# Hybrid encoder layer on one core: head norms for three tiles at a time, rotations four tiles later, a new order on ScalarE and TensorE, and another split of the output projection

## The reference

```
h = x @ w_in                                     # (n, 1024) x (1024, 3328)
qa, ka, va, ga, qb, kb, vb, gb = split(h)        # A: 4 x 512; B: 512, 128, 128, 512
A: 8 heads of 64; q, k rotated by position; three dilated windows as one masked softmax; times silu(ga)
B: qb, kb = axial_rope(rms_norm_per_head(.))     # 8 query heads, 2 key/value heads
   dense softmax attention per 128 queries; times silu(gb)
f = concat(A, B) @ w_out                         # (n, 1024) x (1024, 1024)
y = layer_norm(2 ** 0.25 * x + f)
```

## Time and profile before

| what | us |
|---|---|
| runs shown (median, lowest, highest) | 535.59, 535.48, 537.15 |
| the profiled execution | 535.67 |
| its span, first to last instruction | 533.8 |
| TensorE busy | 442.6 |
| VectorE busy | 321.6 |
| GpSimd busy | 243.9 |
| ScalarE busy | 223.0 |
| mean granted TensorE clock | 0.94 |

### The profile page before, as it was taken

How to read it: one execution, slowest core, us unless ns; L and a number is a source line. 1 busy time by engine, 2 the same in 40 slices (tenths; PEclk the granted TensorE clock), 3 DMA queues, 4 the chain that set the end, 5 groups by cost and what they waited for, 6 DMA issues and landing times.

```text
span 533.8 us, 8372 instructions
## 1 busy us (share of the span) xinstructions
PE 442.6 (83%) x2956; PEld 404.3 (76%) x2956; DVE 321.6 (60%) x858; ACT 223.0 (42%) x515; POOL 243.9 (46%) x358
## 2 busy tenths in 40 slices
PE   2999764099989797999999897999698979897980
PEld 2989764078889787999988886899597868686860
DVE  2585645574556665656566656555366646563997
ACT  3433111024655454465555454456356745341000
POOL 1277666564325354543425355463344945530111
PEclk9999968589999999999999999999899979898895
DMA  7522111012202011020201011002510050010122
GB/s 258 218 62 61 41 38 41 20 39 60 60 20 62 1 40 41 21 60 20 61 10 52 20 41 41 6 16 69 170 60 21 2 177 20 26 55 1 40 92 106
DMA packets 22586, 29.97 MB, mean 56 GB/s; under 512 B 1936, under 2 KB 16400, under 8 KB 22544
## 3 DMA queue, kind: packets, MB, share of 16 engines
q1 hardware_dynamic: 22112, 29.30, 17.2%
q10 hardware_dynamic: 432, 0.13, 0.1%
HBM read 26.28 MB, written 3.15 MB: 55 GB/s over the span
## 4 chain that ended last, share of the span: by engine, by line
DVE 34%; PE 27%; issue 14%; ACT 12%; POOL 9%; DMA 3%; SPq 1%; DVEq 0%; ACTq 0%; POOLq 0%
PE bank L559 6%; PE bank L561 6%; PE bank L560 6%; DVE prob L897 5%; DVE tmp_s L813 4%; PE bank L521 4%; PE bank L634 4%; ACT p_hi L749 4%; DVE h L859 3%; DVE p_lo L905 3%; POOL scr L1066 3%; ACT prob L740 3%; DVE h L834 2%; DVE q_st L911 2%; DVE o_lo L925 2%
## 5 line engine op out<-in xcount | busy, mean ns | idle before, releaser
L559 PE MATMUL bank<-w_hi,t_lo 128*128 128x256 f32 (+1 forms) x528 | 172.0, 326 | 36.7 <-DVE h L834 12.0
L561 PE MATMUL bank<-w_hi,t_hi 128*128 128x256 f32 (+1 forms) x528 | 163.9, 310 | 0.0
L560 PE MATMUL bank<-w_lo,t_hi 128*128 128x256 f32 (+1 forms) x528 | 163.6, 310 | 0.0
L559 PEld LDWEIGHTS bank<-w_hi,t_lo 128*128 128x128 f32 x528 | 104.3, 197 | 46.9 <-DVE h L834 14.1
L740 ACT ACTIVATE prob<-prob,nmax 128x512 f32<-128x512 f32 (+1 forms) x96 | 62.4, 650 | 149.5 <-DVE nmax L897 149.5
L1056 POOL TENSOR_TENSOR w_lo<-raw,w_hi 128x512 fp32r<-128x512 f32 x59 | 76.1, 1290 | 87.5 <-ACT w_hi L694 87.5
L560 PEld LDWEIGHTS bank<-w_lo,t_hi 128*128 128x128 f32 x528 | 104.3, 197 | 4.6
L561 PEld LDWEIGHTS bank<-w_hi,t_hi 128*128 128x128 f32 x528 | 103.9, 197 | 4.4
L905 DVE TENSOR_TENSOR p_lo<-bank,p_hi 128x512 fp32r<-128x512 f32 x80 | 55.2, 690 | 82.9 <-ACT p_hi L749 82.3
L1103 POOL TENSOR_SCALAR prob<-prob,den 128x512 f32<-128x512 f32 (+1 forms) x96 | 59.3, 623 | 84.1 <-DVE den L918 84.1
L694 ACT ACTIVATE w_hi<-raw 128x512 fp32r<-128x512 f32 x67 | 41.7, 626 | 37.5 <-DMA raw<-w_in 31.3
(11 more groups left out here) (78 smaller groups left out, 704.7 us busy)
## 6 DMA issues: line engine op xcount, KB each, us to landing
raw<-w_in SPq DMA_DIRECT2D x51, 256.0 KB, 2.8
raw<-w_out SPq DMA_DIRECT2D x16, 256.0 KB, 4.2
h<-x_prompt SPq DMA_DIRECT2D x10, 256.0 KB, 3.7
y_prompt<-h SPq DMA_DIRECT2D x8, 256.0 KB, 2.0
h<-x_prompt SPq DMA_DIRECT2D x3, 512.0 KB, 8.4
h<-x_sample SPq DMA_DIRECT2D x2, 512.0 KB, 11.2
h<-x_sample SPq DMA_DIRECT2D x4, 256.0 KB, 5.2
y_sample<-h SPq DMA_DIRECT2D x4, 256.0 KB, 2.0
```

The source lines that it names most:

```text
L559: nc.tensor.matmul(out, a_lo, b_hi, start=(m == 0), stop=False)
L560: nc.tensor.matmul(out, a_hi, b_lo, start=False, stop=False)
L561: ins = nc.tensor.matmul(out, a_hi, b_hi, start=False, stop=end)
```

## The change

In the lead-in, GpSimd makes the reciprocal roots of three tiles by one set of six instructions over 6 or 12 columns a row; tile n is rotated in place n + 4, behind the sums of that place; the lead-in has 22 places, so that all four items of GB0 lie in it. In the steps, ScalarE runs the copies of the transposed heads and probabilities ahead of the exponential, and TensorE transposes the probabilities ahead of all its atoms of the step. OB sums three blocks of rows instead of four, OA five instead of four, and four of the five run early for the first four OA items.

```diff
-ALONE = 17
+ALONE = 19
-EARLY_K = 3
+EARLY_K = 4
+OB_TILES, OA_TILES = (4, 5, 6), (7, 0, 1, 2, 3)
...
         def rotations(place):
-            n = len(norms_of)
-            return {0: (), 1: (), 2: (0,), 3: (1, 2)}.get(place, (place - 1,) if place <= n else ())
+            n = place - NORM_TILES - 1
+            return (n,) if 0 <= n < len(norms_of) else ()
...
@@ tensor, step u @@
-                before = (len(plan[u]) + 1) // 2
-                for i, m in plan[u][:before]:
-                    accumulate(i, m)
                 for b in steps[u]:
                     t_batch(b)
                 if LAG <= u < NU + LAG:
                     prob_transposes(u - LAG)
-                for i, m in plan[u][before:]:
+                for i, m in plan[u]:
                     accumulate(i, m)
...
@@ scalar, step u @@
-                if u < NU:
-                    exps(u)
                 for b in steps[u]:
                     t_high(b)
                 if LAG <= u < NU + LAG:
                     prob_high(u - LAG)
+                if u < NU:
+                    exps(u)
...
@@ vector, sums and lead-in @@
-                if n >= 2:
-                    dve.wait_ge(rstd_ready, n - 1)
-                nc.vector.reduce_sum(ssq[:, n % 2, 0:m], heads_of(squares), axis=AX.X).then_inc(summed, 1)
+                g, k = divmod(n, NORM_TILES)
+                if g >= 2:
+                    dve.wait_ge(rstd_ready, g - 1)
+                nc.vector.reduce_sum(ssq[:, g % 2, k, 0:m], heads_of(squares), axis=AX.X).then_inc(summed, 1)
...
+                if KIND[items[i][0]] == NORM:
+                    sums(i)
                 for n in rotations(i):
                     norm_and_rotate(n)
-                if KIND[items[i][0]] == NORM:
-                    sums(i)
...
@@ gpsimd @@
-            def head_rstd(n):
-                m = norm_heads(norms_of[n][0])
-                pool.wait_ge(summed, n + 1)
-                if n >= 2:
-                    pool.wait_ge(products_ready, n - 1)
-                v, y = ssq[:, n % 2, 0:m], scr[:, 0:m]
+            def head_rstd(g):
+                m = norm_heads(norms_of[NORM_TILES * g][0])
+                pool.wait_ge(summed, NORM_TILES * (g + 1))
+                if g >= 2:
+                    pool.wait_ge(products_ready, NORM_TILES * (g - 1))
+                v, y = ssq[:, g % 2, :, 0:m], scr[:, :, 0:m]
...
+                if KIND[items[i][0]] == NORM and i % NORM_TILES == NORM_TILES - 1:
+                    head_rstd(i // NORM_TILES)
                 for n in rotations(i):
                     add_rotation(n)
-                if KIND[items[i][0]] == NORM:
-                    head_rstd(i)
```

More of the change, by code:

```diff
@@ L62 @@
 PRING = 4
+NORM_TILES = 3
 LAG = 3
@@ L185, in build @@
         den = sb("den", [P, 2, TILES])
[L186 to L189, removed]
+        ssq = sb("ssq", [P, 2, NORM_TILES, 4])
+        rstd = sb("rstd", [P, 2, NORM_TILES, 4])
+        scr = sb("scr", [P, NORM_TILES, 4])
+        half = sb("half", [P, NORM_TILES, 4])
         zero = sb("zero", [P, 1])
@@ L253, in build @@
         parts = [4 if KIND[c] == GATE else TILES for c in range(CHUNKS)]
-        k_tiles = [list(range(KT)) if c < IN_CHUNKS else list(range(KT // 2, KT)) if c in (OB0, OB1)
-                   else list(range(KT // 2)) for c in range(CHUNKS)]
+        k_tiles = [list(range(KT)) if c < IN_CHUNKS else list(OB_TILES) if c in (OB0, OB1) else list(OA_TILES)
+                   for c in range(CHUNKS)]
         items = [(c, n) for c in range(OA0) for n in range(parts[c])]
@@ L661, in _ @@
             for i in range(OA_ITEMS, len(items)):
-                for _, m in atoms_of(i, range(EARLY_K, KT // 2) if i < OA_ITEMS + EARLY else None):
+                for _, m in atoms_of(i, range(EARLY_K, len(OA_TILES)) if i < OA_ITEMS + EARLY else None):
                     accumulate(i, m)
@@ L855, in norm_and_rotate @@
                 m = norm_heads(c)
-                dve.wait_ge(rstd_ready, n + 1)
+                g, place = divmod(n, NORM_TILES)
+                dve.wait_ge(rstd_ready, g + 1)
                 src = h[:, t, HOME[c]:HOME[c] + m * HEAD_DIM]
@@ L859, in norm_and_rotate @@
                 after(nc.vector.tensor_tensor(heads_of(src), heads_of(src),
-                                              rstd[:, n % 2, 0:m, None].to_broadcast([P, m, HEAD_DIM]), ALU.mult))
+                                              rstd[:, g % 2, place, 0:m, None].to_broadcast([P, m, HEAD_DIM]), ALU.mult))
                 rotate(src, src, cos[:, k, :], sin[:, k, :], m, HEAD_DIM // 2, ropes.index((c, t)))
@@ L1057, in weights_low @@
                                         ALU.subtract).then_inc(w_lo_pool, 1)
-            def head_rstd(n):
-                m = norm_heads(norms_of[n][0])
-                pool.wait_ge(summed, n + 1)
-                if n >= 2:
-                    pool.wait_ge(products_ready, n - 1)
-                v, y = ssq[:, n % 2, 0:m], scr[:, 0:m]
+            def head_rstd(g):
[4 more added lines that the diff above has]
+                v, y = ssq[:, g % 2, :, 0:m], scr[:, :, 0:m]
                 after(nc.gpsimd.tensor_scalar(v, v, 1.0 / HEAD_DIM, RMS_EPS, ALU.mult, ALU.add))
-                after(nc.gpsimd.tensor_tensor(y, v, half[:, 0:m], ALU.pow))
-                newton(rstd[:, n % 2, 0:m], v, y).then_inc(rstd_ready, 1)
+                after(nc.gpsimd.tensor_tensor(y, v, half[:, :, 0:m], ALU.pow))
+                newton(rstd[:, g % 2, :, 0:m], v, y).then_inc(rstd_ready, 1)
             def add_rotation(n):
@@ L1118, in _ @@
                     weights_low(g)
+                if KIND[items[i][0]] == NORM and i % NORM_TILES == NORM_TILES - 1:
+                    head_rstd(i // NORM_TILES)
                 for n in rotations(i):
                     add_rotation(n)
-                if KIND[items[i][0]] == NORM:
-                    head_rstd(i)
-                if i == TILES:
+                if i == TILES + NORM_TILES + 1:
                     double_keys(0)
-                if i == TILES + 1:
+                if i == TILES + NORM_TILES + 2:
                     split_values(0)
@@ L1146, in _ @@
                 pool.wait_ge(stats_ready, t + 1)
-                nc.gpsimd.tensor_tensor(lnr[:, t, 3:4], lnr[:, t, 2:3], half[:, 0:1], ALU.pow).then_inc(ln_pow, 1)
+                nc.gpsimd.tensor_tensor(lnr[:, t, 3:4], lnr[:, t, 2:3], half[:, 0, 0:1], ALU.pow).then_inc(ln_pow, 1)
 def kernel(**inputs):
```

## The result

| | before | after |
|---|---|---|
| median of the runs (lowest to highest) | 536.35 us (535.48 to 537.15) | 460.3 us (457.19 to 462.06) |
| the profiled execution, its span | 535.67, 533.8 us | 457.19, 455.2 us |
| first score | 119.20 | 91.52 |
| steps, from the first score to the last part | 371.9 us | 320.7 us |
| last part, to the end of the span | 42.7 us | 43.0 us |

The time is 0.8576 of the time before, with a 95% interval of 0.8526 to 0.8626. The forecast was 477 us with a range of 462 to 506; the change gained a little more than the range allowed. In a second set one execution of five took 1083.73 us and is left out as a slow one; the median of the other four is 460.2 us.

The account below looks back on a forecast made before the run. It took a VectorE-GpSimd ring to bound the lead-in, TensorE the steps, VectorE the end. Span 533.8 less 24.2 (lead-in), 13.8 (work), 17 (waits) and 4 (clock) is 474.8, plus 1.9 outside: 477 us, range 462 to 506.

Parts of the forecast that it names:

- lead-in, first score: Before the steps: with roots wanted four places later, 3.25 us a place, first score at 95 instead of 119.2, gaining 24.2 us.
- work that leaves the steps: Steps: two gate items (8.3 us) and eight output atoms (5.5) leave TensorE there, together 13.8 us.
- waits in the steps: Steps: new orders make VectorE's low part some 2 us earlier, removing 17 us of TensorE's waits.
- clock in the steps: Steps: around two TensorE waits the granted clock had fallen, losing 5.1 us; 4 of these come back.
- last part: After the steps: eight more atoms cost nothing, hidden behind VectorE's sums, with cover of 2.1 us at its thinnest.
- I take 17 of the 23.5 us: Steps: of 17 TensorE waits put down to VectorE, 23.5 us in all, 17 us are gained; bounds 0 and 23.5.
- The remaining 11.7 us of idle time I leave: Steps: TensorE's idle time of 35.2 us beyond the 23.5 us of waits on VectorE stays as it was.
- three signs of being wrong: Whole kernel: first score after 105, listed step waits above 15 us, or VectorE's last sums waiting for TensorE.
- Rival 1: Lead-in: VectorE and GpSimd stay a single chain, 4.8 us a place, first score 113, time 495 us; chance 0.13.
- Rivals 2 and 3: Steps: waits stay, 498 us, chance 0.14; or late scaling delays transposes and exponential, slower, up to 573 us, chance 0.04.
- The power was put at 2.2 us: Lead-in: GpSimd's power for a root set of 12 columns, by a straight line from 2 and 4 columns, takes 2.2 us.

Follow-up runs that it names:

- both old orders: Changed kernel with ScalarE's and TensorE's old orders in the steps, lead-in and output split still new: 505.20 us, 0.9435.
- the orders alone: Kernel before with only ScalarE's and TensorE's new orders in the steps, lead-in, roots and output split as before: 493.0 us, 0.9205.

## Why the prediction was right and wrong

By its own sum, for the profiled executions:

| term | predicted | measured |
|---|---|---|
| lead-in, first score | -24.2 | -27.7 |
| work that leaves the steps | -13.8 | in busy time, below |
| waits in the steps | -17 | -25.9 (idle time) |
| clock in the steps | -4 | -6.8, in busy time: the 5.1 of the earlier trace rows and another 1.7 |
| rest of the busy time | not priced | -4.7 (25.3 less 13.8 and 6.8) |
| last part | 0 | +0.3 |
| span | -59.0 | -78.6 |

The steps, all rows between the lead-in and the last part, fell by 51.2 us where the sum has 34.8. The 1.7 us are a third stretch of slow clock in the steps of before, which the earlier trace rows do not show. It lies behind a wait of 4.92 us at 380.94 for a copy on ScalarE that stood behind a late slice (windows of the kernel before):

```profile
377.20:383.20 6.00, 2.26 (x6) 1.78 (x7) 1.63 (x7) 1.46 (x4) 2.06 (x3) 0.82 0.44 161
383.20:389.20 6.00, 6.00 (x32) 5.02 (x31) 2.80 (x7) 4.50 (x12) 4.05 (x5) 0.90 0.28 85
```

The 13.8 us are my count of the work, and the rest of 4.7 us is what that count leaves over. I read it as gaps between matmuls too short to be listed as idle; no run shows that.

**The step that failed** is "I take 17 of the 23.5 us" with "The remaining 11.7 us of idle time I leave", and under it the reading that TensorE works 336.7 of 371.9 us in the steps, "so there it is the bound". I saw that ScalarE and VectorE wait for each other, but priced that ring by the waits that it left on TensorE under four names. With both old orders, taking work from TensorE gave back 2.8 of 13.8 us, so TensorE was not the bound. With the orders alone the steps gave up 43.3 us, against the 21 of waits and clock that I had for them: 30.8 us of idle time, whichever engine its rows name, and 12.5 us of slow clock and other busy time. Of the 11.7 us that I left, the 2.9 us ahead of the last part stand in all of these kernels, and the 4.92 us behind the late slice are 3.36 in the changed kernel. The range failed for the same reason: in the steps its low end let all 23.5 us of waits, the 5.1 of clock and the 13.8 of work go, 42.4 us, and nothing else. None of my three signs of being wrong came, since all three look for a smaller gain.

**The work that leaves the steps** was counted as a gain of its own. It is none while the ring stands (2.8 of 13.8), and with the ring cut the steps of the full change are 7.9 us shorter than those of the orders alone (328.6 to 320.7), not 13.8. Part of the shortfall is the stall of 3.36 us behind the residual loads; there a copy on ScalarE held TensorE up for 1.2 us.

**The lead-in** was right in kind and 3.5 us short. VectorE's squares of the twelve query tiles ran from 39.63 to 74.97, 3.21 us a place where I had 3.25, and VectorE was through place 17 at 78.4 instead of 79.7. Place 18 had no hold-up, and the head copies that TensorE waits for were done at 81.8 where my sum has 84.3. From there TensorE took 9.6 us to the first score; I had 8.8, and 1.9 more for head copies that stick out. The rotations of places 19 to 21, which my sum left out, ran beside TensorE's work; the last ended at 93.0, behind the first score.

Some of the 3.5 us is luck. In the eight profiled executions with this lead-in the first score came at 91.3 to 94.6 us, so the gain is 25 to 28 us; after is one of the two in which TensorE's clock did not fall on the way (last section). The lag and the width are both needed: sets of one tile give 101.3, and three places instead of four 98.9.

**Rival 1** fell, and the power shows why (timelines of VectorE and GpSimd after):

```profile
46.84 2.29 POOL L1067 TENSOR_TENSOR scr<-ssq,half 128x12 f32<-128x12 f32 x1
...
47.98 0.42 DVE L846 TENSOR_TENSOR tanh<-h 128x256 f32<-128x256 f32 x1 [0.44 <-ACT h L720]
48.43 0.42 DVE L850 TENSOR_REDUCE ssq<-tanh 128x4 f32<-128x256 f32 x1
...
81.84 1.28 POOL L1057 TENSOR_TENSOR w_lo<-raw,w_hi 128x512 fp32r<-128x512 f32 x1
81.88 1.53 DVE L860 TENSOR_TENSOR h<-h,rstd 128x256 f32<-128x256 f32 x1
```

VectorE's square runs its 0.42 us in the middle of a power of 2.29, and the multiplications at 58.50 and 78.28 ran inside such powers and took 0.41 and 0.42; beside a weight slice one takes 1.53. The Trainium skill, "SBUF — State Buffer", section "Who interferes with whom", has such a pair shut each other out. By the weight slice the trace agrees (1.53 beside 1.28, against 0.42 alone); for the power it shows no such hold-up.

**Rivals 2 and 3** fell. The waits went, all of them. The scaling is late for the transposes once, by 0.4 us, and the exponential's place behind the copies costs nothing that shows. The power was put at 2.2 us and took 2.28. **The last part** went as predicted: TensorE worked to about 32 us behind its start, and VectorE waited for it only at its first sum there, 1.9 us as before.

## What to carry to other kernels

When two engines wait for each other once in every step, price the ring by its turn, not by the waits that it leaves on a third engine, however busy that one looks; the test is to take work from the third engine and see whether the step gets shorter. In an order written by hand, put what another engine waits for ahead of what waits for that engine. Work moved out of a stage is a gain only in a stage that follows that work, and in a queue that is worked through in order, loads that are large, or must themselves wait for something, belong behind the small ones that an engine is about to need.

## What the runs showed of the hardware that I had not expected

GpSimd's power took 0.71, 1.01, 1.35 and 2.28 us for 2, 4, 6 and 12 columns, by my estimate about 0.16 us a column over some 0.4; the other five instructions of a set took 0.19 to 0.31 us on average at any of these widths. Three tiles in one power thus saved 0.75 us of three at 1.01, and the other instructions saved more.

One stop of TensorE can cost its clock or not. In the eight profiled executions with the changed lead-in TensorE stops for 2.57 to 2.68 us at about 82 us, and the granted clock between 81 and 94 us is 1.00 in two of them (after and both old orders), 0.87 in five and 0.74 in one. The first score came at 91.5 and 91.3 us in the two, at 92.8 to 94.6 in the six. What decides it is open. The clock behind the stop in the second set's profile of the changed kernel (its windows; stop of 2.60 us ending at 82.00, first score at 92.82):

```profile
82.00:93.00 11.00, 11.00 (x57) 9.69 (x58) 9.72 (x19) 3.26 (x7) 7.09 (x7) 0.85 0.26 72
```
